# Loading X in column quarters, later places in the mixers' chains, and gated linear scores in two banks

## The reference

```python
# first_block, for l in 0, 1
h = rms_norm(x, norm_w[l]); p = h @ w_in[l]            # 2048 x 6668
oa = sliding_window_sink_attention(rope(rms_norm(qa)), rope(rms_norm(ka)), va, sinks) * silu(za)
ob = conformer_conv_module(ub, ...) * silu(zb)         # 31 taps along time, layer norm, pointwise matmul
oc = rms_norm(gated_deltanet(qkv_c, b_c, a_c, ...)) * silu(zc)
x = x + concatenate([oa, ob, oc]) @ w_out[l]
# second_block, for layer in 0, 1
x = x + hybrid_mixer(rmsnorm(x), w_in_2, ...)          # differential attention, gated linear, retention
x = x + conv_ffn(rmsnorm(x), w_up, conv_w, conv_b, w_down)
# end
return rmsnorm(x, final_g)
```

## Time and profile before

| | |
|---|---|
| median of 3 runs | 3596.53 us (3594.49 to 3596.84) |
| profiled execution | 3592.43 us, span 3590.6 us |
| mean granted TensorE clock | 0.984 |
| TensorE busy | 3448.8 us (96%), 16074 matmuls |
| VectorE, ScalarE, GpSimd busy | 2285.3 (64%), 1852.1 (52%), 157.4 us (4%) |
| DMA | 578.5 MB, 161 GB/s over the span |

### The profile page before, as it was taken

The page is one execution under the profiler, slowest core; times in us unless marked ns, Lnnn a source line. Parts: engine busy times, 40 slices in busy tenths (PEclk is TensorE's granted clock), DMA queues, the critical chain, the costliest instruction groups (busy, mean ns, idle before and its releaser), DMA issues.

```text
span 3590.6 us, 41541 instructions
## 1 busy us (share of the span) xinstructions
PE 3448.8 (96%) x16074; PEld 2776.4 (77%) x16074; DVE 2285.3 (64%) x3130; ACT 1852.1 (52%) x2526; POOL 157.4 (4%) x243
## 2 busy tenths in 40 slices
PE   7989999989999999999999999999999999999998
PEld 5767678767678777788888888887777888888886
DVE  4866565956655666556666666666665566666665
ACT  4464645464645355655454455553565555445444
POOL 3014000023000000000000000000000000000000
PEclk9999999999999999999999999999999999999999
DMA  7434356534356345455655655653444565565564
GB/s 205 135 110 134 100 163 188 145 101 136 99 171 194 98 134 141 138 189 176 198 184 181 197 185 179 193 171 102 149 135 152 188 194 182 187 194 182 186 195 153
DMA packets 399092, 578.51 MB, mean 161 GB/s; under 512 B 25473, under 2 KB 222585, under 8 KB 398256
## 3 DMA queue, kind: packets, MB, share of 16 engines
q1 hardware_dynamic: 392544, 557.93, 50.7%
q0 software_dynamic: 5904, 16.75, 1.6%
q10 hardware_dynamic: 448, 1.18, 0.1%
HBM read 570.78 MB, written 4.98 MB: 160 GB/s over the span
## 4 chain that ended last, share of the span: by engine, by line
PE 82%; DVE 11%; ACT 5%; issue 2%; DMA 1%; DVEq 0%; ACTq 0%; SPq 0%
PE PS L708 79%; DVE WL L1850 3%; PE PS L705 3%; DVE ZA L2041 2%; ACT WH L1314 1%; DVE AR L1990 1%; DMA RAW<-in_w_in 0%; DVE AR L2314 0%; ACT L1577 0%; ACT AR L1659 0%; DVE SM L2247 0%; DVE AR L2245 0%; DMA X<-in_x 0%; ACT AR L1577 0%; ACT AR L1340 0%
## 5 line engine op out<-in xcount | busy, mean ns | idle before, releaser
L1850 DVE TENSOR_TENSOR WL<-RAW,WH 128x1024 fp32r<-128x1024 f32 x1056 | 1292.4, 1229 | 958.1 <-ACT WH L1314 955.4
L1314 ACT ACTIVATE WH<-RAW 128x1024 fp32r<-128x1024 f32 x1056 | 1106.0, 1055 | 977.7 <-PE PS L708 575.7
L708 PE MATMUL PS<-WH,Ah 128*128 128x512 f32 x3520 | 1426.9, 405 | 41.9 <-DVE WL L1850 34.1
L708 PE MATMUL PS<-WL,Ah 128*128 128x512 f32 x3520 | 1383.8, 393 | 0.0
L708 PE MATMUL PS<-WH,Al 128*128 128x512 f32 x3520 | 1382.9, 393 | 0.0
L708 PEld LDWEIGHTS PS<-WH,Ah 128*128 128x128 f32 x3520 | 668.9, 190 | 212.7 <-issue 37.9
L708 PEld LDWEIGHTS PS<-WL,Ah 128*128 128x128 f32 x3520 | 667.5, 190 | 144.3
L708 PEld LDWEIGHTS PS<-WH,Al 128*128 128x128 f32 x3520 | 669.5, 190 | 138.2 <-issue 6.8
L708 PE MATMUL PS<-WH,Zh 128*128 128x512 f32 x704 | 278.4, 395 | 0.6
L708 PE MATMUL PS<-WL,Zh 128*128 128x512 f32 x704 | 274.3, 390 | 0.0
L708 PE MATMUL PS<-WH,Zl 128*128 128x512 f32 x704 | 274.2, 389 | 0.0
(11 more groups left out here) (320 smaller groups left out, 2160.9 us busy)
## 6 DMA issues: line engine op xcount, KB each, us to landing
RAW<-in_w_in SPq DMA_DIRECT2D x368, 512.0 KB, 3.7
RAW<-in_w_up SPq DMA_DIRECT2D x704, 256.0 KB, 3.1
RAW<-in_w_down SPq DMA_DIRECT2D x176, 512.0 KB, 4.0
RAW<-in_w_out SPq DMA_DIRECT2D x64, 512.0 KB, 3.6
RAW<-in_w_o SPq DMA_DIRECT2D x64, 512.0 KB, 3.7
RAW<-in_w_in SPq DMA_DIRECT2D x64, 256.0 KB, 3.1
AR<-in_c POOLq DMA_DIRECT2D x2, 1600.0 KB, 7.4
AR<-bias_scratch POOLq DMA_DIRECT2D x16, 192.0 KB, 4.7
```

Of the source, the lines that this page charges most:

```text
L708: return T.matmul(o, lhs, rhs, start=start, stop=stop, skip_group_check=True)
L1314: act(WH[:, j % NW, 0:n], raw_view(j), ACT.Copy).then_inc(*w_hi())
L1850: tt(WL[:, j % NW, 0:w], raw_view(j), WH[:, j % NW, 0:w].bitcast(F32), SUB).then_inc(*w_lo())
```

## The change

Three parts, in one edit.

1. Round 0 goes quarter by quarter. X comes in four column quarters of 512 KB with a semaphore each, issued by SyncE before weight tiles 0, 1, 2 and 3. Quarter c starts 2c places later, the squares and their sum come behind what the matmuls need, and the first tile follows place 2 (before: place 3), so `set_up` comes one tile later.
2. In the first block, all of `mixer_c` from the norms on, and the end of `mixer_b`, come two places later on all engines. `mixer_a` works in halves (one token tile each), over more places, and its five turns come four places later than that.
3. In `gla`, chunks gv and ga come before gqk, and the gates' logs start on ga alone. The two row halves of the scores go to two banks, without the wait between them; both token tiles of a level are scored at once. A level takes three places (26 in all). VectorE multiplies queries and keys in one instruction, and copies both tiles under the mask in one.

```diff
-C2CH = [("gqk", [(3072, 512)]), ("gv", [(3584, 512)]), ("ga", [(4608, 32)]), ("gr", [(4096, 512)]),
+C2CH = [("gv", [(3584, 512)]), ("ga", [(4608, 32)]), ("gqk", [(3072, 512)]), ("gr", [(4096, 512)]),
...
 # TensorE, prepare(r, c)
                 if r == 0:
-                    T.wait_ge(x_in, 32)
+                    for _ in range(2 * c):
+                        yield
+                    T.wait_ge(x_in[c], 16)
                     if c == 0:
                         T.wait_ge(*u_dve.at("prm0"))
-                    turn_x(c, 0, 4 + c)
-                    yield
-                    T.wait_ge(*p_gt.at(gt_index(r, c, 0)))
-                    turn_x(c, 1, 4 + c)
-                    yield
                 else:
                     yield
                     T.wait_ge(*x_added.at(x_index[r] + c))
-                    if c > 1:
-                        T.wait_ge(*p_gt.at(gt_index(r, c - 2, 1)))
-                    for q in R2:
-                        turn_x(c, q, 4 + 2 * (c % 2) + q)
-                    yield
+                if c > 1:
+                    T.wait_ge(*p_gt.at(gt_index(r, c - 2, 1)))
+                for q in R2:
+                    turn_x(c, q, 4 + 2 * (c % 2) + q)
+                yield
                 yield
...
 # VectorE, prepare(r, c)
+                for _ in range(2 * c + 1 if r == 0 else 2):
+                    yield
+                if c == 3 and r > 0:
+                    sum_squares(r)
+                for q in R2:
+                    gain_x(r, c, q, 4 + 2 * (c % 2) + q)
+                if c == 3 and r == 0:
+                    sum_squares(r)
+                yield
...
 # mixer_b, TensorE (ScalarE: 32 to 34, VectorE: two more yields)
-                for _ in range(31):
+                for _ in range(33):
                     yield
                 T.wait_ge(*b_dve.at(m("t29_3")))
...
 # mixer_c, TensorE, ScalarE and VectorE
                 yield from e.until("qkv0", "qkv1", "qkv2")
+                yield
+                yield
...
 # mixer_a, TensorE (ScalarE: 6 to 9)
                 yield from e.until("qa0", "qa1", "pw")
-                for _ in range(7):
+                for _ in range(11):
                     yield
...
 # mixer_a, VectorE
+                for t in R2:
+                    V.wait_ge(*a_act.at(m(f"sq{t}")))
+                    red(KSS[:, 16 * t:16 * t + 16], SQT[:, t, :].rearrange("p (h d) -> p h d", d=64), AX.X, ADD).then_inc(*a_dve(m(f"ss{t}")))
+                    yield
+                yield
                 V.wait_ge(*a_act.at(m("rs")))
-                tt(qv, qv, KSS.unsqueeze(2).broadcast_to([128, 32, 64]), MUL).then_inc(*a_dve(m("qn")))
-                yield
+                for t in R2:
+                    qv = QK[:, t, :].rearrange("p (h d) -> p h d", d=64)
+                    tt(qv, qv, KSS[:, 16 * t:16 * t + 16].unsqueeze(2).broadcast_to([128, 16, 64]), MUL).then_inc(*a_dve(m(f"qn{t}")))
+                    yield
...
 # gla, TensorE
+                def scores(q, k, tiles, names):
+                    for i in R2:
+                        at = slice(64 * i, 64 * i + 64)
+                        for c in R2:
+                            for t, (jt, it) in enumerate(tiles):
+                                o = 256 * c + 128 * t
+                                ins = mm(PS[:, names[2] + i, o:o + 128], k[at, c, 128 * jt:128 * jt + 128], q[at, c, 128 * it:128 * it + 128])
+                        ins.then_inc(*g_pe(m(names[i])))
...
-                for i in range(17):
+                for i in range(26):
                     for d in R2:
-                        n, half = divmod(i - d, 2)
+                        n, k = divmod(i - d, 3)
...
+                        elif k == 2:
+                            T.wait_ge(*g_dve.at(m(f"qk{d}{n}")))
+                            tiles = ((0, 0), (1, 1)) if n < 7 else ((0, 1),) if d == 0 else ((1, 0),)
+                            scores(two(QKE[d][:, 0, :]), two(QKE[d][:, 1, :]), tiles, (f"sc{d}{n}x", f"sc{d}{n}", 4 + 2 * d))
...
 # gla, VectorE
-                            tt(QE[:, d, :], flat(GQ), EE[:, d, :], MUL).then_inc(*g_dve(m(f"qe{d}{n}")))
-                            tt(KE[:, d, :], flat(GK), EE[:, d, :], MUL).then_inc(*g_dve(m(f"ke{d}{n}")))
+                            tt(QKE[d], GQK, EE[:, d, :].unsqueeze(1).broadcast_to([128, 2, 512]), MUL).then_inc(*g_dve(m(f"qk{d}{n}")))
...
+                                pred(blocks, mask.unsqueeze(1).unsqueeze(1).broadcast_to([128, 4, 2, 128]),
+                                     pv.rearrange("p b (c t n) -> p (b c) t n", t=2, n=128)).then_inc(*g_dve(m(f"pa{d}{n - 1}")))
...
 # SyncE
-            for t in R2:
-                Y.dma_start(X[:, t, :], a["x"][0, 128 * t:128 * t + 128, :]).then_inc(x_in, 16)
+            def load_x(c):
+                o = slice(512 * c, 512 * c + 512)
+                Y.dma_start(X[:, :, o], a["x"][0, :, o].rearrange("(t p) n -> p t n", p=128)).then_inc(x_in[c], 16)
+
+            load_x(0)
             for j, (mat, segs, width, row, kp) in enumerate(plan):
+                if 1 <= j < 4:
+                    load_x(j)
```

More of the change, by code:

```diff
@@ L353, in program @@
         m_hi, m_lo = count("merged_hi"), count("merged_lo")
-        ident_in, x_in, prm0_in, prm_in = sem("ident_in"), sem("x_in"), sem("prm0_in"), sem("prm_in")
+        ident_in, prm0_in, prm_in = sem("ident_in"), sem("prm0_in"), sem("prm_in")
+        x_in = [sem(f"x{c}_in") for c in range(4)]
         const_in, hot_in, scr_in = sem("const_in"), sem("hot_in"), sem("scr_in")
@@ L426, in program @@
         items = [(t, h0) for t in (1, 0) for h0 in range(0, 12, 2)]
-        aa_, ap, ad = ["sq", "ln", "rs"], [f"qt{c}" for c in range(5)], ["ss", "qn"]
+        aa_, ap, ad = ["sq0", "sq1", "ln", "rs"], [f"qt{c}" for c in range(5)], ["ss0", "ss1", "qn0", "qn1"]
         ad += [f"{n}{t}" for t in R2 for n in ("qw", "kw")] + [f"rope_{n}{t}" for t in R2 for n in "abcdef"]
@@ L458, in program @@
         lev_pe, lev_act, lev_dve = [], [], []
-        for i in range(17):
+        for i in range(26):
             for d in R2:
-                n, half = divmod(i - d, 2)
+                n, k = divmod(i - d, 3)
+                if k == 0 and 1 <= n < 9:
+                    lev_dve += [f"pa{d}{n - 1}"]
                 if 0 <= n < 8:
-                    lev_pe += [f"cs{d}{n}"] if half == 0 else [f"sc{d}{n}{k}{x}" for k in range(2 if n < 7 else 1) for x in ("x", "")]
-                    lev_act += [f"ex{d}{n}"] if half == 0 else []
-                    lev_dve += [f"qe{d}{n}", f"ke{d}{n}"] if half == 0 else [f"pa{d}{n}{k}" for k in range(2 if n < 7 else 1)]
+                    lev_pe += [f"cs{d}{n}"] if k == 0 else [f"sc{d}{n}x", f"sc{d}{n}"] if k == 2 else []
+                    lev_act += [f"ex{d}{n}"] if k == 1 else []
+                    lev_dve += [f"qk{d}{n}"] if k == 1 else []
         ga_ = ["le", "za0", "ze0", "za1", "ze1", "zl0", "zl1"] + lev_act
@@ L1108, in m @@
                     return f"{l}.{s}"
-                yield from e.until("ga", "gqk")
+                yield from e.until("ga")
                 T.wait_ge(*n_act.at(f"2.{l}.out1"))
@@ L1328, in prepare @@
             def prepare(r, c):
-                if 0 < r < 6:
+                if r == 0:
+                    for _ in range(2 * c + 1):
+                        yield
+                    A.wait_ge(x_in[c], 16)
+                elif r < 6:
                     yield
-                if r == 0:
-                    A.wait_ge(x_in, 32)
-                else:
+                if r > 0:
                     A.wait_ge(*x_added.at(x_index[r] + c))
@@ L1505, in mixer_b @@
                         scale=P(("bcw", l), 30 * 4 + c)).then_inc(*b_act(m(f"id{c}")))
-                for _ in range(32):
+                for _ in range(34):
                     yield
@@ L1641, in mixer_a @@
                 act(KSS, KSS, ACT.Exp, scale=-0.5).then_inc(*a_act(m("rs")))
-                for _ in range(6):
+                for _ in range(9):
                     yield
@@ L1693, in gla @@
                     yield
+                yield from e.until("gqk")
                 yield
-                for i in range(17):
+                for i in range(26):
                     for d in R2:
-                        n, half = divmod(i - d, 2)
-                        if 0 <= n < 8 and half == 0:
+                        n, k = divmod(i - d, 3)
+                        if 0 <= n < 8 and k == 1:
                             A.wait_ge(*g_pe.at(m(f"cs{d}{n}")))
                             if n > 0:
-                                A.wait_ge(*g_dve.at(m(f"ke{d}{n - 1}")))
+                                A.wait_ge(*g_dve.at(m(f"qk{d}{n - 1}")))
                             act(EE[:, d, :], bank(4 + 2 * d), ACT.Exp).then_inc(*g_act(m(f"ex{d}{n}")))
@@ L2325, in gla @@
                 yield
+                yield from e.until("gqk")
                 V.wait_ge(*g_dve.at(m("la1")))
+                V.wait_ge(*g_pe.at(m("dg")))
```

(5 more changed lines are left out.)

123 lines of the change are left out of this document (43 added, 80 removed).

## The result

The changed kernel takes 3574.23 us (median of 4 runs, 3569.35 to 3575.14) beside 3596.05 us for the kernel before on the same chip: a ratio of 0.9937, 95% interval 0.9920 to 0.9954, 22 us. The profiled execution took 3569.35 us (span 3567.4), 23.1 us less than that of before. Forecast were 38 us, and 3558 us for the median. The sign and the range (3537 to 3578) held, but 16 of the 38 us are missing, and the time lies nearer to two of the rivals (3573 and 3571) than to the forecast.

The account below looks back on a forecast made before the run. TensorE, busy 96% of 3590.6 us, was taken to bound the kernel; only its stalls, matmuls beside the weights and low-clock stretches could be saved. Opening -10.0, mixers -13.3, heads -14.6 sum to -37.9 us: 3558 us, range 3537 to 3578.

Parts of the forecast that it names:

- the three stretches named: Where TensorE's waits lie: the opening, the mixers of the two first layers, and the gated linear heads.
- one packet for one: Opening: DMA queues alternate packet by packet, so 2 KB packets of X let prm0 land at 6.3 instead of 9.36.
- (a): Mixers, ScalarE's first square: two more weight tiles fill TensorE's 6.12 us stop, net 3.05 us saved.
- (b): Mixers, mean of mixer_b: the 5.12 us wait for the last tap row goes, plus 1.7 at full clock.
- (c): mixer_a: halves and four more places remove four stalls (1.26 to 3.85 us), given back waiting for GpSimd at "ta".
- TTM comes sooner by 9.85 - 5.45 = 4.4: Mixers at "ta": GpSimd's result TTM, its chain length unchanged, comes 4.4 us sooner; part of -5.9 and -7.4 us.
- a wait for L2352's successor: Gated heads' levels: TensorE waiting for this line, or L2338's successor, would show the prediction wrong.
- each wait has about 1.1 us of cover: Gated heads: VectorE needs 9.1 of 14.1 us per three places, leaving each wait about 1.1 us of cover.
- −1.7 a layer for the wait at the diagonal: Gated heads: the gates' logs start 8 tiles sooner, so the diagonal's 1.67 us wait goes.
- the two row halves overlap: Rival, gated heads' scores: different banks let the halves run side by side, -3.3 us a layer, 3551 us; chance 0.12.
- the drain comes with the change of halves: Rival, gated heads: the gap comes from changing row halves, not the semaphore; Part 3 +1.9 - 1.7, 3573 us; chance 0.12.
- the rival with the short opening: Rival: opening bound by prm0 and row loads, -6, mixers -4, heads -14.6: 3571 us; chance 0.12.

Follow-up runs that it names:

- e7: The kernel after with the edits to mixer_a undone (7 places for 11, whole operations for halves): 3567.80 us.
- e9: The kernel after with score merges ahead of decayed products, 15 places for 12 ahead of "ta", and mixer_a's edits undone: 3553.90 us (3540.98 with them).
- e4: The kernel after with VectorE's score merges ahead of the decayed products in each place of the gated heads: 3558.17 us.
- e6: The kernel after with TensorE's own wait put back between the scores' row halves, which stay in two banks: 3596.98 us.
- e1 to e3: The kernel before with one part alone changed: the opening 3590.16 us, the first blocks' mixers 3587.89 us, the gated heads 3591.62 us.
- e3: The kernel before with the gated heads alone changed: 3591.62 us, ratio 0.9995.

## Why the prediction was right in sign and range, and 16 us off

*What bounds the kernel, and the clock.* Right. Every gain and loss in these runs was in the three stretches named, and what the table leaves out of the span is 1632.6 to 1633.1 us in all fourteen profiles. Behind each stall of 4 us or more in before and after stood slow passes (2.06 for 1.05 us).

*Part 1, −10.0 forecast.* The first matmul was put near 14 and came at 14.47; tile 6 was put at 37.0 and came at 38.34; the stretch to number 193 fell by 10.2 in this profile and by 8.9 over the eleven kernels that have the edit. The term was right within 1.1 us, and that the one profile has 10.2 for 10.0 is partly luck: prm0 landed at 7.87, not 6.3, and raw tile 3, put at 12.6, was asked for at 14.35. DMA queues in after, 5 to 6 us (packets, MB, share):

```profile
q1 hardware_dynamic: 200, 0.38, 99.2%
q10 hardware_dynamic: 19, 0.01, 2.9%
```

The step rested on one packet for one, as 219 to 213 in the earlier trace rows. Between 3 and 4 us the queues still move 104 and 96, but in this microsecond 200 and 19. If the queues took turns packet for packet, as the profile counts packets, the small one would have kept pace while it had any; its block was not complete until 7.87, so here the trace does not agree with that reading of the rule cited there. The page (DMA: Bandwidth & Descriptors, Queues, rings and completion order, in the Trainium skill) has a packet hold several descriptors, and no row says whether the profile counts the same thing. What held the small queue back stays open.

*Part 2, −13.3 forecast.* The steps (a) and (b) are as told: the 6.12 us wait fell to 2.30, the wait for the tap rows is gone, and in layer 0 nothing above 0.6 us came in its place. (c), that mixer_a's smoothing would not be saved because TensorE would come early to the transposes and wait for GpSimd, is what happened: e7 shows the smoothing worth nothing, e9 that it is worth 10 us once the wait is removed. Two things in it were off. It counted the short waits for VectorE's weight tiles (1.26 and 1.14 in before) as removed, with nothing but the wait at "ta" to follow; but TensorE, now early, found a later tile (the 70th, where it had waited for the 63rd and 64th) not ready and lost 4.50 us there, 5.61 in layer 1. Forecast were 11 to 13 us of waiting at "ta"; 7.27 and 6.49 came, and with the late tile 11.8 and 12.1, so this moved the wait rather than adding to it. What cost the gain is the term "TTM comes sooner by 9.85 - 5.45 = 4.4". In layer 0 GpSimd's last loads were issued at 305.42 for 315.38, 10.0 us sooner, and the opening alone had given 10.2 in this profile: its chain started 1.7 us sooner than by the opening and took 65.1 us for 63.2. In layer 1 it took 64.6 for 60.6. The prediction had the length unchanged. Over the kernels with and without the edits the stretches fell by 4.9 and 5.2 us, 10 for the 13 forecast; in the profile pair itself by 6.6.

*Part 3, −14.6 forecast, 6.7 measured.* Here most of the gap lies: the stretches with and without the edit differ by 3.4 and 3.3 us. The prediction had called a wait for L2352's successor a sign that it is wrong, and that wait came. The step that failed is "each wait has about 1.1 us of cover". It summed VectorE's own work against the places and left out what that work waits for: ScalarE's exponential, and the chunk's evacuation ahead of it in ScalarE's queue. e4 prices this at 12 us. A second term failed too, −1.7 a layer for the wait at the diagonal. That wait is gone, but at its first products of 64 rows TensorE now waits about as long, in layer 0 for ScalarE's copy of the keys, whose chunk gqk now comes last (after, layer 0; 1.61 in layer 1, for VectorE's logs):

```profile
1151.23 1.68 PE L712 MATMUL PS<-AR 64*128 64x128 f32 x16 [1.50 <-ACT AR L1464]
```

So 3 of these 3.4 us came back. Against both stands a term that gave more than forecast, the scores themselves. With the order mended Part 3 is worth 19. A level of both directions fell by 1.2 us, where the waits less one more change of pattern were counted at 0.73; over 16 such levels that makes up for 7 to 8 us. Part of it is that the two row halves overlap, a rival with a chance of 0.12 and a price of 3.3 us a layer: a place of two tiles fell by 0.59 where two waits of 0.235, 0.47, were counted. That rival is true, and true together with the forecast's own cause, not in its place, since taking the wait out is what lets the halves overlap (e6). The other rival, that the drain comes with the change of halves, is refuted by e6. That it had put the time at 3573, and the rival with the short opening at 3571, both nearer to the 3574 measured than the forecast, is chance: the runs show the mechanism of neither (the opening gave 9 us, not 6, and the mixers 10, not 4).

*The sum.* −8.9, −10.1 and −6.7 from the groups of the table are 25.7 us, beside 23.1 in the profiles and 22 in the runs. Of the missing 16 us about 8 are in Part 3, some 3 in Part 2 and 1 in Part 1; the other 4 lie between the groups of the table and the runs, and no run places them. The parts were added as if in series. e1 to e3 show that they are not: alone they bring 10 us, in part since VectorE's tap rows stand between opening and mixers and do not come earlier with the opening.

## What to carry to other kernels

When the slack of an engine is summed over places, ask also in which order it does its work there and what each piece waits for: one instruction that TensorE needs, queued behind one that waits for a third engine, made stalls of 4.35 us that an average over places did not show, and moving it forward cost nothing. A wait for a long chain on another engine (here 60 to 66 us on GpSimd) turns into waiting what TensorE gains after the chain has started, so edits there should be judged together with the place of that wait: the same smoothing was worth nothing with twelve places and 10 us with fifteen. Where matmuls use half the rows, put the halves into different banks, with no wait between them, and issue them in turn.

## What the hardware showed that was not expected

Sixteen fp32 passes of 64 rows and 128 columns took 2.37 us with a wait of TensorE for itself between the halves, 1.71 us as eight and eight without it, and 1.16 us in turn. Two queues that shared the DMA engines packet for packet with packets of 6.9 KB on average in one of them (219 to 213 between 4 and 8 us) did not with packets of 2 KB (200 to 19 between 5 and 6 us). And mixers with unchanged code took up to 3.6 us longer in one kernel's profile than in another's, as much as some parts of this change bring; in e3 three short waits had become one of 6.65 us, and the 11 runs showed the loss too.
